# Walking the common unit of weights by column block instead of by k in a two-block transformer kernel

## The reference, cut to what matters

```
# block 1
h = rms_norm(r, g_mix);  z = h @ w_in                  # q, k, v, conv parts, gates
attn = moba_attention(q, k, v)                         # causal, 8 heads of 128
y_attn = attn @ w_attn_out;  y_conv = (c_b * conv3(c_c * c_x)) @ w_conv_out
r = r + (sigmoid(g_a) * y_attn + sigmoid(g_c) * y_conv) @ w_o
h = rms_norm(r, g_mlp);  r = r + square(relu(h @ w_up)) @ w_down
h = rms_norm(r, g_ple);  r = r + sigmoid(h @ w_ple_gate) * (p @ w_ple_proj)
# block 2, with 16 meta tokens put in front
u = rms_norm(h, mix_pre) @ conv_w_in + b;  u = a * sigmoid(g)
u = layer_norm(depthwise_conv31(u));  u = silu(u) @ conv_w_out + b
h = h + rms_norm(u, mix_post)
u = rms_norm(h, ffn_pre);  u = (silu(u @ w_gate) * (u @ w_up)) @ w_down
out = (h + rms_norm(u, ffn_post))[16:]
```

## Time and profile before

| | |
|---|---|
| median of 3 runs | 2592.4 us (2590.39 to 2595.18) |
| profiled execution, its own time | 2591.07 us |
| its span, first to last instruction | 2588.8 us |
| mean granted clock of TensorE | 0.993 |
| PE busy | 2540.1 us, 98% |
| DVE busy | 1756.0 us, 68% |
| ACT busy | 1273.7 us, 49% |
| POOL busy | 459.2 us, 18% |
| share of 16 DMA engines, weight queue | 58% |

### The profile page before, as it was taken

The page is one execution under the profiler, slowest core; times in us unless marked ns, Lnnn a source line. Parts: engine busy times, 40 slices in busy tenths (PEclk is TensorE's granted clock), DMA queues, the critical chain, the costliest instruction groups (busy, mean ns, idle before and its releaser), DMA issues.

```text
span 2588.8 us, 43837 instructions
## 1 busy us (share of the span) xinstructions
PE 2540.1 (98%) x14943; PEld 2248.4 (87%) x14943; DVE 1756.0 (68%) x2120; ACT 1273.7 (49%) x1604; POOL 459.2 (18%) x300
## 2 busy tenths in 40 slices
PE   8999999999999999999999999989899999999998
PEld 7888788888888888888888899978788888888887
DVE  6578875577765665665667879985766556665665
ACT  5456555554544444444445544454654444444444
POOL 4034410001100000000011268862400000000003
PEclk9999999999999999999999999999999999999999
DMA  6655456665566665566655555536466656666653
GB/s 199 202 174 172 147 185 193 189 193 179 170 187 195 189 190 188 180 198 189 187 185 179 179 157 161 163 94 205 140 195 184 195 179 194 193 188 188 190 181 130
DMA packets 497408, 465.27 MB, mean 180 GB/s; under 512 B 14476, under 2 KB 494214, under 8 KB 497286
## 3 DMA queue, kind: packets, MB, share of 16 engines
q1 hardware_dynamic: 496816, 463.92, 58.0%
q10 hardware_dynamic: 516, 0.38, 0.1%
HBM read 462.15 MB, written 2.10 MB: 179 GB/s over the span
## 4 chain that ended last, share of the span: by engine, by line
PE 91%; DVE 4%; issue 2%; ACT 1%; POOL 1%; DVEq 0%; ACTq 0%; POOLq 0%
PE gp L396 54%; PE gp L399 25%; PE gp L405 3%; PE gp L588 2%; PE gp L590 2%; PE gp L589 2%; DVE wlo L1195 1%; POOL acc L1739 1%; PE xp L606 1%; POOL sq L1736 0%; DVE xp L1517 0%; ACT whi L718 0%; PE xp L633 0%; DVE s L1206 0%; DVE s L1474 0%
## 5 line engine op out<-in xcount | busy, mean ns | idle before, releaser
L1195 DVE TENSOR_TENSOR wlo<-stage,whi 128x1024 fp32r<-128x1024 f32 x811 | 1014.1, 1266 | 674.0 <-ACT whi L718 667.4
L718 ACT ACTIVATE whi<-stage 128x1024 fp32r<-128x1024 f32 x876 | 915.7, 1057 | 967.3 <-PE gp L399 723.8
L396 PE MATMUL gp<-A,whi 128*128 128x512 f32 x3968 | 1315.8, 394 | 7.0 <-DVE A L1598 7.0
L399 PE MATMUL gp<-A,wlo 128*128 128x256 f32 x3200 | 898.7, 281 | 0.0
L396 PEld LDWEIGHTS gp<-A,whi 128*128 128x128 f32 x3968 | 741.2, 188 | 170.1 <-issue 8.1
L396 PE MATMUL gp<-B,whi 128*128 128x512 f32 x2496 | 872.1, 394 | 9.6 <-DVE B L1568 7.9
L399 PE MATMUL gp<-B,wlo 128*128 128x256 f32 x2496 | 700.1, 280 | 0.0
L399 PEld LDWEIGHTS gp<-A,wlo 128*128 128x128 f32 x3200 | 604.3, 189 | 0.0
L396 PEld LDWEIGHTS gp<-B,whi 128*128 128x128 f32 x2496 | 468.1, 188 | 116.5 <-issue 10.2
L399 PEld LDWEIGHTS gp<-B,wlo 128*128 128x128 f32 x2496 | 472.4, 189 | 0.1
L1736 POOL TENSOR_TENSOR sq<-r 128x512 f32 (+1 forms) x32 | 38.9, 1215 | 814.6 <-DVE r L1427 756.4
(11 more groups left out here) (289 smaller groups left out, 1418.9 us busy)
## 6 DMA issues: line engine op xcount, KB each, us to landing
stage<-in_w_in SPq DMA_DIRECT2D x160, 512.0 KB, 4.6
stage<-in_w_up SPq DMA_DIRECT2D x128, 512.0 KB, 3.8
stage<-in_w_down SPq DMA_DIRECT2D x128, 512.0 KB, 4.2
stage<-in_ffn_w_gate SPq DMA_DIRECT2D x88, 512.0 KB, 4.5
stage<-in_ffn_w_up SPq DMA_DIRECT2D x88, 512.0 KB, 4.5
stage<-in_ffn_w_down SPq DMA_DIRECT2D x88, 512.0 KB, 4.5
stage<-in_conv_w_in SPq DMA_DIRECT2D x64, 512.0 KB, 4.1
stage<-in_w_o SPq DMA_DIRECT2D x32, 512.0 KB, 4.5
```

The lines of the kernel that those rows point to most:

```text
L396: nc.tensor.matmul(bank.rearrange("p (a t) -> p a t", a=2), hi, both_parts(M, kt), start=first, stop=False)
L399: done = nc.tensor.matmul(bank[:, T:2 * T], lo, M[:, kt, 0:T], start=False, stop=last)
L718: nc.scalar.activation(whi[:, slot, :], stage[:, slot, :], ACT.Copy).then_inc(hi_ready, 1)
L1195: nc.vector.tensor_tensor(wlo[:, slot, :], stage[:, slot, :], whi[:, slot, :].bitcast(F32), ALU.subtract).then_inc(lo_ready, 1)
```

## The change

In the common form (neither `single` nor `hi_first`) the loops over k and m change places. Before, the unit was walked k by k, and for each k the two column blocks with hi and lo each. After, all four k of column block 0 are done, hi and lo in turn, and then all four of column block 1. The operand is waited for once per unit, for all its four k tiles. The two other forms keep their code, moved into an `else`. The signals at the end of a unit and the hooks stay. Line numbers after step's head shift by up to 12; the new matmuls stand on L392 (hi) and L394 (lo).

```diff
+                    if not single and not hi_first:
+                        if ready:
+                            pe.wait_ge(ready[0], ready[1] + ready[2] * (u + 1))
+                        for m in range(2):
+                            bank = gp[:, 2 * j + m, :]
+                            for k in range(4):
+                                kt, c = kt0 + 4 * u + k, k * HPW + m * P
+                                nc.tensor.matmul(bank.rearrange("p (a t) -> p a t", a=2), whi[:, slot, c:c + P], both_parts(M, kt),
+                                                 start=u == 0 and k == 0, stop=False)
+                                done = nc.tensor.matmul(bank[:, T:2 * T], wlo[:, slot, c:c + P], M[:, kt, 0:T], start=False,
+                                                        stop=u == units - 1 and k == 3)
+                    else:
                         for k in range(4):
-                        if single and u == 0 and k < 2:
-                            pe.wait_ge(ready[0], ready[1] + k + 1)
-                        elif ready and k % 2 == 0:
-                            pe.wait_ge(ready[0], ready[1] + ready[2] * u + ready[2] // 2 * (k // 2 + 1))
...
```

More of the change, by code:

```diff
@@ L384, in step @@
                         pe.wait_ge(evacuated, XSLOTS + hp - 1)
-                    for k in range(4):
-                        if single and u == 0 and k < 2:
-                            pe.wait_ge(ready[0], ready[1] + k + 1)
-                        elif ready and k % 2 == 0:
-                            pe.wait_ge(ready[0], ready[1] + ready[2] * u + ready[2] // 2 * (k // 2 + 1))
-                        kt = kt0 + 4 * u + k
-                        first, last = u == 0 and k == 0, u == units - 1 and k == 3
+                    if not single and not hi_first:
+                        if ready:
+                            pe.wait_ge(ready[0], ready[1] + ready[2] * (u + 1))
@@ L392, in step @@
                         for m in range(2):
-                            c = k * HPW + m * P
-                            hi, lo = whi[:, slot, c:c + P], wlo[:, slot, c:c + P]
                             bank = gp[:, 2 * j + m, :]
[L396 to L399, removed]
@@ L400, in step @@
-                    if hi_first:
-                        pe.wait_ge(lo_ready, n0 + u + 1)
-                        for k in range(4):
+                            for k in range(4):
[5 more added lines that the diff above has]
+                    else:
+                        for k in range(4):
+                            if single and u == 0 and k < 2:
+                                pe.wait_ge(ready[0], ready[1] + k + 1)
+                            elif ready and k % 2 == 0:
+                                pe.wait_ge(ready[0], ready[1] + ready[2] * u + ready[2] // 2 * (k // 2 + 1))
+                            kt = kt0 + 4 * u + k
+                            first, last = u == 0 and k == 0, u == units - 1 and k == 3
@@ L403, in step @@
                             for m in range(2):
                                 c = k * HPW + m * P
-                                done = nc.tensor.matmul(gp[:, 2 * j + m, T:2 * T], wlo[:, slot, c:c + P], M[:, kt0 + 4 * u + k, 0:T],
-                                                        start=False, stop=u == units - 1 and k == 3)
+                                hi, lo = whi[:, slot, c:c + P], wlo[:, slot, c:c + P]
+                                bank = gp[:, 2 * j + m, :]
+                                nc.tensor.matmul(bank.rearrange("p (a t) -> p a t", a=2), hi, both_parts(M, kt),
+                                                 start=first, stop=False)
@@ new lines, in step @@
+                                if not hi_first:
+                                    done = nc.tensor.matmul(bank[:, T:2 * T], lo, M[:, kt, 0:T], start=False, stop=last)
+                        if hi_first:
+                            pe.wait_ge(lo_ready, n0 + u + 1)
+                            for k in range(4):
+                                for m in range(2):
+                                    c = k * HPW + m * P
+                                    done = nc.tensor.matmul(gp[:, 2 * j + m, T:2 * T], wlo[:, slot, c:c + P], M[:, kt0 + 4 * u + k, 0:T],
+                                                            start=False, stop=u == units - 1 and k == 3)
```

## The result

| | before | after |
|---|---|---|
| median of the runs | 2592.4 us (2590.28 to 2595.18, 5 runs) | 2606.21 us (2605.44 to 2610.51, 5 runs) |
| ratio to before | | 1.0057, 95% interval 1.0045 to 1.0068 |
| profiled execution, span | 2591.07, 2588.8 us | 2608.15, 2605.8 us |
| PE busy | 2540.1 us | 2554.6 us |
| up1 (B), 32 units | 88.74 us | 90.45 us |

What follows compares the result with a forecast made beforehand. TensorE's list of matmuls was taken as the bound (PE busy 98% of the span). Terms 0 (order) + 0 (dropped waits) + 1.6 (out2) + 0.2 (back2) = +1.8 us on the 2592.4 median gave 2594; range 2584 to 2607.

Steps and rivals of the forecast that it cites:

- The order of the matmuls: In 708 rewritten units, bank changes less often and operand moves with each pair; taken as 0 us from the all-hi-first form.
- ends of -25 and +33 us: Bounds for the new order over all rewritten units: conv2's 12 ns excess per matmul, or its ratio 1.107.
- the waits' 1.8: Forecast cost of one wait per unit for all four k: +1.6 us at out2, +0.2 in back2.
- The rival with the long rhythm: 224 short B units go long at 54 ns each, 12.1 us; with 1.8, 2606 us. Slower by rhythm or ratio: 0.21.
- The rule held against it: Argument that B stays short: every B stage that follows a full stage has the short rhythm.
- The rate looks like the tile's: Argument against A units gaining 14 ns: the all-hi-first form, another order, gives A's rate too.
- The coarser wait: Units wait for all four k: PE starts out2 1.58 us later, back2's third unit 0.2 us later, other stages unaffected.
- its term of 1.0 to 2.8: At out2's start, the shift with half clock ending at the same moment or later; taken +1.6 us, the shift alone.
- nothing makes the 1.58 us good: At out2, the later start lies on the chain of waits, so all that follows moves by 1.58 us.
- The dropped waits: Each of 708 units loses its second operand wait, before k = 2: 0 to 7 us possible, taken as 0.
- The bank rival: If changing bank costs 12 ns, six changes fewer per unit over 708 units save 51 us, 2543 us; chance 0.03.

Runs made afterwards that it cites:

- e5: Kernel before with one wait per unit, first four pairs of a unit sent to bank 0, last four to bank 1 (wrong sums): 2592.4 us against 2591.81.
- e3: Changed kernel's order and wait only in units whose operand is A, B units as before: 2608.89 us, ratio 1.006.
- e4: Changed kernel's order and wait only in units whose operand is B, A units as before: 2594.25 us, ratio 1.0015.
- e7: Kernel before with one wait per unit, only the operand walking on with each pair (wrong products): 2608.61 us against 2591.81.
- w288: Kernel before with only A's rows wider, 2 x 288 columns instead of 2 x 272, qk held in acc: 2600.55 us, ratio 1.0037.
- c_old: Kernel before with each A tile's 512 columns read as one run instead of two of 256 (wrong product): 2606.61 us.
- c_new: Changed kernel with each A tile's 512 columns read as one run instead of two of 256 (wrong product): 2596.66 us.
- e1: Kernel before, old order, with only the change's coarser wait (one per unit, for all four k): 2591.99 us against 2590.43, ratio 1.0005.
- k64: Changed kernel with one small 64-column matmul before attn_out, each up, back0 and back1: 2603.49 us, ratio 1.0046.
- k128: Changed kernel with one small 128-column matmul before attn_out, each up, back0 and back1: 2598.42 us, ratio 1.0027.

## Why the prediction was wrong

- **The order of the matmuls: wrong, and this is the step that failed.** The term of the sum was put at 0 "from the nearest row: hi-first", between ends of -25 and +33 us. The measured value, about +12 us by the medians (13.8 less the waits' 1.8) and 15.3 by the stage times (A 5.1 and B 10.2), lies between those ends, so the bounds held and the choice didn't. The hi-first form has the other extreme of bank order, but it holds the operand for two matmuls just as the common form does. It bounded the bank only, which e5 then showed to be free. The text itself said that two things move, bank and operand, and then priced both by a row that varies one. conv2 was the only row with a walking operand, and it stood at one of the ends.
- **The rival with the long rhythm: right in its time (2606), partly by luck.** 192 of the 224 units it named went long, 10.2 us by the stage table. The other 32, gate's, were mostly long before, and out2's 32, counted as long, were short; the two mistakes nearly cancel in the count. Its 12.1 + 1.8 us lacked A's 5.1 and met the measured median because not all of B changed and because out2's wait, half clock and back2 came to little. Its reason was half right. Something outside B's own code does pick the rhythm, but the changed addresses act through A and not through B (e3, e4). The rule held against it, that a stage that follows a full stage is short, was drawn from a kernel in which every A stage ran alike. What reached B from A may have been one state, seen many times, and not as many witnesses.
- **A's rate: missed.** No rival had A slower by a fixed 13 ns (5.1 us over 396 units). "The rate looks like the tile's" was wrong twice: the order changes it (e7) and so do the rows' width and the reading (w288, c_old, c_new).
- **The coarser wait: right.** +1.58 us at out2 forecast, 7.89 to 9.47 us measured; +0.2 in back2, 0.2 measured; all other stages unharmed. e1 has +1.6 us by medians, with no change inside its interval. The half clock cost 0.55 us more than the plain shift, inside its term of 1.0 to 2.8. That nothing makes the 1.58 us good was not so in this execution, where the layer norm came 0.8 us sooner.
- **The dropped waits: right.** e1 has them dropped in the old order, and its units keep 2.773 and 2.787 us. Met waits cost nothing that shows.
- **The bank rival: wrong, as weighed.** With one bank for eight matmuls nothing changed (e5). The granted clock of the changed kernel is again 1.00 from 46.5 to 1517 us, where the mean over so long a stretch hides the two short ones at half clock, in ccx and gate:

```profile
46.50:1517.00 1470.50, 1459.48 (x8343) 1273.11 (x8341) 991.66 (x1066) 722.31 (x881) 163.10 (x125) 1.00 0.58 182
```

The sum as measured between the two profiled executions: A 5.1 and B 10.2 us, both from the order; out2 1.3; back2 -0.9, with its wait of 0.2 in it; ccx 1.5, gate 1.0, conv2 -1.3 and up0 0.2. That is 17.1, and the span grew by 17.0. The medians differ by 13.8; stretches at half clock, which come in some executions and not in others, don't fall out of a comparison of one execution with one.

What stays open is why: what in TensorE makes a B unit 2.773 or 2.827 us and an A unit 2.787 or 2.800 was not found. Shown is only that the operand's order and place select A's rate, and that what comes just ahead of a stage can select B's.

## What to carry to other kernels

When a change moves several streams of an operation at once (bank, weights, moving operand), a neighbouring row prices only the streams that differ in it; ask for each stream which row varies it alone. On a kernel that is bound by a dense stream of matmuls, read unit times as distances between stage starts, to the nanosecond: a stream can settle into one of several steady rhythms 2% apart, and what selects the rhythm can lie in the stage before. A change that looks neutral for its own code can then cost or save time a stage later, and a forecast should hold the price of every steady stage in the other rhythm in its range.

## What the runs showed of the hardware that was not expected

- One stream of the same matmuls on the same tiles runs at 2.773 or 2.827 us per 16 matmuls, for whole stages of 32 units. One matmul of 64 or 128 columns ahead of the stage, which makes it 0.1 us longer, can change that (k64, k128). In up0 and gate the rhythm also changes in mid-stage, at the first unit of a step, where PE loses a few hundredths to some tenths of a us.
- The long rhythm is a sequence of steps that repeats every three pairs of matmuls (1060 ns), though nothing in the program repeats every three pairs.
- With two runs of 256 columns per tile, 1088 bytes apart, holding the moving operand for two column blocks gave 2.787 us a unit and walking it 2.800 (e7). Set 1152 bytes apart and held: 2.800 (w288, with the caution said there). One run, held: 2.800, and walked: 2.787 (c_old, c_new).
- Filling one PSUM bank with eight matmuls in a row or changing it with each pair is the same to under 1 ns a matmul (e5 against e1, one profiled execution each).
